# The four DeltaNet rounds of a two-layer trunk, laid out anew between the weight units

## The chip, the core and the metric

One core of one Trainium2 chip runs the whole kernel. The time is device microseconds of one execution; the median of three runs before is 2995.3 us (2992.6 to 3002.73). Engines: TensorE (PE), VectorE (DVE), ScalarE (ACT), GpSimd (POOL), and SP, which asks for the weights.

## The reference

A decoder trunk of two layers over 256 tokens and 2048 features, float32. Layer 0 mixes with mLSTM and retention, layer 1 with a gated DeltaNet; each layer ends with a SwiGLU, and each product with weights is a (256 x 2048 or wider) by (weights) matmul. The change lies in layer 1's mixer. Cut to what matters:

```python
proj = h @ w_in                                   # q, k, v (8192 columns), z, gates
qkv = silu(causal_depthwise_conv(qkv, conv_w))    # width 4
q, k = l2norm(q) * GD ** -0.5, l2norm(k)          # 16 heads of 128; v has 32
decay = exp(where(causal, g_cum[:, None] - g_cum[None, :], -inf))
a = where(strict, (k_beta @ k.T) * decay, 0)
u, w = triangular_solve(a, [v * beta, k_beta * exp(g_cum)])
attn = where(causal, (q @ k.T) * decay, 0)
# state from chunk to chunk: v_new = u - w s; out = q_g s + attn v_new
o = head_rmsnorm(out) * norm_w * silu(z);  return o @ w_out
```

## The kernel before

**Weights.** All weight products are made of 928 units. A unit is 256 rows x 512 columns of a weight matrix. SP loads it into one of four buffers `wraw`; ScalarE rounds it into `whi` (L948), VectorE takes the rest into `wlo` (L1372), and TensorE makes 12 matmuls of 512 columns: eight with `whi` (L536, L537), four with `wlo` (L542). ScalarE and VectorE may be three units ahead of TensorE at most. Eight units make a block of 512 output columns in layer 1's input projection; it has 24 blocks, 192 units, of which 16 blocks give k, q and v and 8 give z.

**Rounds.** The DeltaNet part is done for 8 value heads at a time, in four rounds, between the units of this projection. Round r begins at unit `ROUND_AT[r]` and has slots s = 0, 1, 2, ...: the function `gdn(r, s)` of each engine holds what the slot does. TensorE runs slot s right after unit `ROUND_AT[r] + s`. ScalarE and VectorE run it after their part of the unit two later (`AHEAD = 2`). So the order of work on every engine is written out by hand, and a slot that waits on another engine holds back the units behind it.

**What a round does, in slots of before.** 0 to 4: k's columns are turned (`conv_transposes`, L589), tapped (L1169) and convolved (`conv`, L1719, twelve VectorE operations), decays are summed (L749), exponentiated (L1186) and turned (L756, L1190); k is turned back (`token_major`, L742), its squares summed (L1180), k k^T formed (L763) and masked (L1729). 5, 6: the triangular systems A (`system`, L1736). 7, 12, 17: the convolutions of q and both halves of v. 8 to 19: the inversion of the 32 x 32 diagonal blocks (`leaf`, L1754 and L1757, 31 steps of two small VectorE operations, each step behind the one before; start L1743, end L1761, L1764). 9, 11, 14: q k^T, its mask, and its product into `ET` (L1809). 22 to 27: two levels of block inversion (`level_q`, `level_t`, `level_tt`, all through `per_head`, L769; copies L1204; subtractions L1769). 28 to 36: values, state and outputs, squares of the output (L1290), its norm (L1863). Both PSUM tensors `aux[0]` and `aux[1]` are shared by all of this; the four other banks hold the weight products. GpSimd makes the level masks (`level_part`, L490), zeroes T and TT, copies the leaves into T (L504), and stores each round's output to HBM; ScalarE loads it back in the last round. z blocks follow: `z_out` applies SiLU, `gate(n)` on VectorE multiplies it with the round's output.

## Time and profile before

| | |
|---|---|
| median of three runs | 2995.3 us |
| profiled execution | 2994.38 us, span 2992.6 us |
| TensorE / VectorE / ScalarE / GpSimd busy | 96% / 53% / 46% / 4% |
| chain that ended last | TensorE 84%, VectorE 9%, ScalarE 4% |
| mean granted TensorE clock | 0.981 of full speed |

Read it so: busy time is the union of an engine's instructions; a TensorE matmul's end is modelled, so its row says 0.39 us while the next starts 0.23 later. The granted clock is a share of 2.4 GHz. Idle time of an engine other than TensorE costs nothing by itself here.

### The profile page before, as it was taken

What the parts mean: (1) busy time and instruction counts of PE and PEld (TensorE: products, weight loads), DVE (VectorE), ACT (ScalarE), POOL (GpSimd) and SP (SyncE); (2) the same over time, 40 slices, a digit from 0 to 9 for tenths busy, and PEclk for the clock granted to TensorE, in tenths of its full rate; (3) what the DMA queues carried; (4) which work ended last, traced back from release to release, by engine and by line L of the source; (5) the groups of instructions that cost most, each with busy time, mean ns of one, the idle gap of its engine ahead of it and who ended that gap; (6) DMA issues with size and microseconds to landing.
All of it is one profiled execution on the core that took longest, in us unless ns stands there. A gap on an engine that the chain in (4) does not pass through costs nothing.

```text
span 2992.6 us, 37024 instructions
## 1 busy us (share of the span) xinstructions
PE 2860.9 (96%) x13396; PEld 2369.6 (79%) x13396; DVE 1586.1 (53%) x1934; ACT 1378.9 (46%) x1874; POOL 118.3 (4%) x75
## 2 busy tenths in 40 slices
PE   8999989999999999998989898899999999999998
PEld 6788768888888788876868787787888888887886
DVE  4544555544544454467484847655545544544444
ACT  5444445444444344464555637454445444443433
POOL 0000000000000000020120111000000000000000
PEclk9999989999999999999999999999999999999999
DMA  7464546666666566544434434454566666665654
GB/s 237 144 192 145 156 142 188 190 189 189 188 191 182 176 189 189 172 141 120 120 113 127 114 109 130 150 167 153 185 185 195 189 190 189 189 189 176 191 191 145
DMA packets 261265, 502.74 MB, mean 168 GB/s; under 512 B 20112, under 2 KB 20368, under 8 KB 260624
## 3 DMA queue, kind: packets, MB, share of 16 engines
q1 hardware_dynamic: 259504, 494.73, 55.0%
q0 software_dynamic: 816, 3.15, 0.3%
q10 hardware_dynamic: 816, 3.15, 0.3%
q8 instruction: 80, 1.31, 0.2%
q14 instruction: 49, 0.40, 0.0%
HBM read 495.72 MB, written 5.24 MB: 167 GB/s over the span
## 4 chain that ended last, share of the span: by engine, by line
PE 84%; DVE 9%; ACT 4%; issue 2%; DVEq 2%; DMA 0%; ACTq 0%; SPq 0%
PE acc L536 25%; PE acc L542 25%; PE acc L537 25%; PE aux L769 4%; DVE wlo L1372 2%; PE aux L589 2%; DVE arena L1757 1%; DVE arena L1754 1%; DVE const L1719 1%; DVE arena L1719 1%; ACT whi L948 1%; DVEq L1756 1%; DVEq L1723 0%; ACT arena L1290 0%; ACT aux L1180 0%
## 5 line engine op out<-in xcount | busy, mean ns | idle before, releaser
L1372 DVE TENSOR_TENSOR wlo<-wraw,whi 128x1024 fp32r<-128x1024 f32 x928 | 1151.7, 1246 | 1151.3 <-ACT whi L948 1143.6
L948 ACT ACTIVATE whi<-wraw 128x1024 fp32r<-128x1024 f32 x928 | 975.1, 1061 | 1102.4 <-PE acc L542 1048.4
L536 PE MATMUL acc<-whi,hT_hi 128*128 128x512 f32 x2624 | 1047.3, 399 | 7.5 <-ACT whi L948 7.1
L537 PE MATMUL acc<-whi,hT_lo 128*128 128x512 f32 x2624 | 1029.7, 392 | 0.0
L542 PE MATMUL acc<-wlo,hT_hi 128*128 128x512 f32 x2624 | 710.6, 393 | 42.7 <-DVE wlo L1372 42.7
L542 PEld LDWEIGHTS acc<-wlo,hT_hi 128*128 128x128 f32 x2624 | 492.9, 189 | 157.5 <-DVE wlo L1372 55.4
L536 PEld LDWEIGHTS acc<-whi,hT_hi 128*128 128x128 f32 x2624 | 497.7, 190 | 110.6 <-issue 8.8
L537 PEld LDWEIGHTS acc<-whi,hT_lo 128*128 128x128 f32 x2624 | 497.6, 190 | 102.7 <-issue 1.9
L536 PE MATMUL acc<-whi,arena 128*128 128x512 f32 x1088 | 431.1, 396 | 13.8 <-ACT whi L948 5.3
L537 PE MATMUL acc<-whi,arena 128*128 128x512 f32 x1088 | 428.9, 394 | 0.0
L542 PE MATMUL acc<-wlo,arena 128*128 128x512 f32 x1088 | 295.2, 393 | 0.0
L536 PEld LDWEIGHTS acc<-whi,arena 128*128 128x128 f32 x1088 | 206.6, 190 | 59.3 <-issue 5.5
L537 PEld LDWEIGHTS acc<-whi,arena 128*128 128x128 f32 x1088 | 206.8, 190 | 45.4
L542 PEld LDWEIGHTS acc<-wlo,arena 128*128 128x128 f32 x1088 | 205.8, 189 | 45.3
L769 PEld LDWEIGHTS aux<-arena,arena 128*128 128x128 f32 x960 | 114.0, 193 | 5.3 <-issue 2.6
L769 PE MATMUL aux<-arena,arena 128*128 128x128 f32 x960 | 114.6, 276 | 1.1 <-ACT arena L1255 1.1
L478 POOL COPY x<-xs 128x1024 f32 x16 | 19.2, 1198 | 2257.2 <-DVE xs L1410 2257.2
L964 ACT ACTIVATE arena<-acc,rstd 128x512 f32<-128x512 f32 x120 | 75.5, 684 | 15.6 <-PE acc L542 11.4
L589 PE MATMUL aux<-const,arena 128*128 128x128 f32 x240 | 32.4, 284 | 16.8 <-DVE arena L1524 9.8
L490 POOL TENSOR_TENSOR arena<-arena,const 128x1024 f32<-128x1024 f32 x16 | 41.8, 2635 | 137.0 <-DVE arena L1736 136.1
L589 PEld LDWEIGHTS aux<-const,arena 128*128 128x128 f32 x240 | 28.7, 146 | 21.9 <-DVE arena L1524 10.3
L1754 DVE TENSOR_TENSOR arena<-arena,arena 128x126 f32<-128x126 f32 (+22 forms) x124 | 39.7, 320 | 7.2 <-issue 0.4
(231 smaller groups left out, 1190.6 us busy)
## 6 DMA issues: line engine op xcount, KB each, us to landing
wraw<-in_l_w_in SPq DMA_DIRECT2D x304, 512.0 KB, 3.8
wraw<-in_l_w_gate SPq DMA_DIRECT2D x176, 512.0 KB, 3.7
wraw<-in_l_w_up SPq DMA_DIRECT2D x176, 512.0 KB, 3.7
wraw<-in_l_w_down SPq DMA_DIRECT2D x176, 512.0 KB, 4.4
wraw<-in_l_w_out SPq DMA_DIRECT2D x96, 512.0 KB, 4.6
o_rounds<-arena POOLq DMA_DIRECT2D x3, 1024.0 KB, 4.9
arena<-o_rounds ACTq DMA_DIRECT2D x3, 1024.0 KB, 5.1
x<-in_x SPq DMA_DIRECT2D x4, 512.0 KB, 6.0
```

The source lines that it names most:

```text
L490: nc.gpsimd.tensor_tensor(dst[:, c], A_[:, c], mask, ALU.mult).then_inc(part_set, 1)
L536: nc.tensor.matmul(pair[m], hi[:, k, tok], wh, start=first, stop=False)
L537: nc.tensor.matmul(pair[m], lo[:, k, tok], wh, start=False, stop=False)
L542: mm = nc.tensor.matmul(pair[m], hi[:, k, m * P:(m + 1) * P], wl, start=False, stop=k_last)
L589: mm = nc.tensor.transpose(dst[:, t * SEQ + m * P:t * SEQ + (m + 1) * P], src(m, t), ident)
L769: mm = nc.tensor.matmul(to[:, head(h)], left(h), right(h), start=True, stop=True)
L948: nc.scalar.activation(whi[:, s, :], wraw[:, s, :], ACT.Copy).then_inc(hi_done, 1)
L964: a = nc.scalar.activation(dst(m), acc[parity][:, m, :], func, scale=rstd[:, m:m + 1])
L1372: V.tensor_tensor(wlo[:, s, :], wraw[:, s, :], whi[:, s, :].bitcast(F32), ALU.subtract).then_inc(lo_done, 1)
L1719: a = V.scalar_tensor_tensor(dst[:, t, lag:], src[:, t * SEQ:(t + 1) * SEQ - lag], conv_w[:, w, CW - 1 - lag:CW - lag], dst[:, t, lag:], o ...
L1754: V.tensor_tensor(p, lead[:, j, j + 1:].unsqueeze(2).to_broadcast([P, rows, cols]), leaf_t[:, j:j + 1, 0:cols].to_broadcast([P, rows, cols ...
L1756: dve.drain()
```

## The change

Rounds begin at units 20, 57, 94 and 131 and have up to 43 slots, so a round's last slots lie over the first ones of the next. The order of the projected blocks, and of the convolutions, becomes k, first half of v, q, second half of v. In the first half of a round only k and the first half of v are convolved; the leaf inversion takes slots 10 to 20 with three steps each and nothing beside them. The convolution of q moves to slot 21, that of the second half of v to 27, q k^T and its mask to 25, the product into ET to 26. The level products now all use `aux[1]`, one a slot, each behind the subtraction of the one before; `aux[0]` is used for q and v beside them. GpSimd makes its second level mask after it has copied the leaves. The mask of k k^T moves from slot 4 to 6, A from 5 and 6 to 7 and 8. Values, state and output follow at 32 to 36, squares at 38, the root at 40, the norm at 41. The outputs of rounds 0 and 1 are loaded back to other addresses, at slots 9 and 27 of the last round, the transposed outputs of the rounds lie in another order, and the output projection takes rows of its weights in the order of `OUT1_W`. z blocks 1 and 3 are read at other units (147, 165 for 150, 163), and the first four gates follow `Z_GATED`. The core of the diff:

```diff
 Z_BLOCK = 16
+Z_GATED = [146, 149, 164, 167, 173, 181, 189]
 
 GDN_GATE_STEPS = ["raw", "exp", "log1p", "sums", "sums_exp", "neg"]
 GATE_AT = {s: i + 1 for i, s in enumerate(GDN_GATE_STEPS)}
 
 
-ROUND_AT = [23, 59, 95, 131]
-ROUND_SLOTS = 40
-
-K, Q, V0, V1 = range(4)
+ROUND_AT = [20, 57, 94, 131]
...
-TOK_AT = counts(K, Q, V0, V1)
+TOK_AT = counts(K, V0, Q, V1)
 GRAM_AT = counts("kk", "kq")
 ROOT_AT = counts("k", "q")
 LEAF_AT = counts("T", "TT")
 PART_AT = counts((32, 0), (32, 1), (64, 0), (64, 1))
-LEVEL_PSUM = counts("q32_0", "q32_1", "T32_0", "TT32_0", "T32_1", "TT32_1", "q64_0", "q64_1", "TT64_0", "TT64_1")
+LEVEL_PSUM = counts("q32_0", "q32_1", "TT32_0", "T32_0", "TT32_1", "T32_1", "q64_0", "TT64_0", "q64_1", "TT64_1")
 LEVEL_COPY = counts("q32_0", "q32_1", "q64_0", "q64_1")
-LEVEL_SUB = counts("T32_0", "TT32_0", "T32_1", "TT32_1", "TT64_0", "TT64_1")
+LEVEL_SUB = counts("TT32_0", "T32_0", "TT32_1", "T32_1", "TT64_0", "TT64_1")
 END_PSUM = counts("vn0", "s", "o0", "ks", "qs", "vn1", "o1")
...
-        o_z = [at(0, [P, M, HV * GD]), at(8 * KB, [P, M, HV * GD]), at(40 * KB, [P, M, HV * GD]), o_r]
+        o_z = [qkv[:, :, 0:HV * GD], qkv[:, :, HV * GD:], at(40 * KB, [P, M, HV * GD]), o_r]
         o_dram = nc.dram_tensor("o_rounds", (SEQ, VH * GD), F32, kind="Internal").ap()
 
         O_ORDER = [0, 2, 1, 3]
+        O_AT = [3, 1, 2, 0]
+        OUT1_W = [HV * r + t for r in O_ORDER for t in range(HV)]
+        OUT1_O = [HV * O_AT[r] + t for r in O_ORDER for t in range(HV)]
         oT_hi = at(0, [P, 2 * KT, SEQ], F32R)
...
-                pool.wait_ge(diag_set, r + 1)
-                pool.drain()
-                level_part(1, B64)
                 pool.wait_ge(leaf_set, LEAF_AT(r, "T"))
                 for b in range(4):
                     pool.drain()
                     a = nc.gpsimd.tensor_copy(T[quarter(b), :, :, quarter(b)].rearrange("p c h j -> p (c h) j"), leaf_T[quarter(b), :, :])
                 a.then_inc(t_in, 1)
+                pool.wait_ge(diag_set, r + 1)
                 pool.drain()
+                level_part(1, B64)
...
                     if r:
-                        pe.wait_ge(end_act, END_ACT(r - 1, "vn1"))
+                        pe.wait_ge(end_dve, END_DVE(r - 1, "o1"))
                     else:
                         pe.wait_ge(gate_step, GATE_AT["sums_exp"])
+                    decays(0, aux[1])
+                    if r:
+                        pe.wait_ge(end_act, END_ACT(r - 1, "vn1"))
                     conv_transposes(K, aux[0])
-                    if r:
-                        pe.wait_ge(end_dve, END_DVE(r - 1, "o1"))
-                    decays(0, aux[1])
-                if s == 1:
+                if s == 2:
                     pe.wait_ge(d_exp, D_AT(r, 0))
                     decays(1, aux[1])
-                if s == 2:
+                if s == 4:
                     pe.wait_ge(d_exp, D_AT(r, 1))
                     decays_turned(0, aux[1])
-                if s == 3:
                     pe.wait_ge(conv_sum, TOK_AT(r, K))
                     token_major(K, aux[0])
+                if s == 5:
                     pe.wait_ge(et_copy, D_AT(r, 0))
                     products(4, aux[1])
-                if s == 4:
+                if s == 7:
                     pe.wait_ge(gram_mask, GRAM_AT(r, "kk"))
                     decays_turned(1, aux[1])
-                if s == 5:
-                    pe.wait_ge(et_copy, D_AT(r, 1))
-                    conv_transposes(Q, aux[1])
-                if s == 9:
                     pe.wait_ge(tok_copy, TOK_AT(r, K))
-                    token_major(Q, aux[0])
-                    pe.wait_ge(conv_sum, TOK_AT(r, Q))
-                    products(0, aux[1])
-                if s == 10:
-                    pe.wait_ge(tok_copy, TOK_AT(r, Q))
                     conv_transposes(V0, aux[0])
                 if s == 13:
-                    pe.wait_ge(gram_mask, GRAM_AT(r, "kq"))
-                    conv_transposes(V1, aux[1])
-                if s == 15:
                     pe.wait_ge(conv_sum, TOK_AT(r, V0))
                     token_major(V0, aux[0])
-                if s == 21:
+                if s == 15:
                     pe.wait_ge(tok_copy, TOK_AT(r, V0))
-                    token_major(V1, aux[0])
-                if s == 22:
-                    pe.wait_ge(conv_sum, TOK_AT(r, V1))
+                    conv_transposes(Q, aux[0])
+                if s == 23:
+                    pe.wait_ge(et_copy, D_AT(r, 1))
                     pe.wait_ge(part_set, PART_AT(r, (32, 0)))
                     pe.wait_ge(tt_in, r + 1)
                     level_q(B32, 0, aux[1])
-                if s == 23:
-                    pe.wait_ge(tok_copy, TOK_AT(r, V1))
+                if s == 24:
                     pe.wait_ge(part_set, PART_AT(r, (32, 1)))
-                    level_q(B32, 1, aux[0])
-                if s == 24:
+                    pe.wait_ge(lev_copy, LEVEL_COPY(r, "q32_0"))
+                    level_q(B32, 1, aux[1])
+                    pe.wait_ge(conv_sum, TOK_AT(r, Q))
+                    token_major(Q, aux[0])
+                if s == 25:
                     pe.wait_ge(t_in, r + 1)
-                    pe.wait_ge(lev_copy, LEVEL_COPY(r, "q32_0"))
+                    pe.wait_ge(lev_copy, LEVEL_COPY(r, "q32_1"))
+                    level_tt(0, aux[1])
+                    pe.wait_ge(tok_copy, TOK_AT(r, Q))
+                    products(0, aux[0])
+                if s == 26:
+                    pe.wait_ge(lev_sub, LEVEL_SUB(r, "TT32_0"))
                     level_t(0, aux[1])
-                    pe.wait_ge(lev_copy, LEVEL_COPY(r, "q32_1"))
-                    level_tt(0, aux[0])
-                if s == 25:
+                    pe.wait_ge(gram_mask, GRAM_AT(r, "kq"))
+                    conv_transposes(V1, aux[0])
+                if s == 27:
                     pe.wait_ge(lev_sub, LEVEL_SUB(r, "T32_0"))
+                    level_tt(1, aux[1])
+                if s == 28:
+                    pe.wait_ge(lev_sub, LEVEL_SUB(r, "TT32_1"))
                     level_t(1, aux[1])
-                    pe.wait_ge(lev_sub, LEVEL_SUB(r, "TT32_0"))
-                    level_tt(1, aux[0])
-                if s == 26:
+                if s == 29:
                     pe.wait_ge(part_set, PART_AT(r, (64, 0)))
                     pe.wait_ge(lev_sub, LEVEL_SUB(r, "T32_1"))
                     level_q(B64, 0, aux[1])
-                    pe.wait_ge(part_set, PART_AT(r, (64, 1)))
-                    pe.wait_ge(lev_sub, LEVEL_SUB(r, "TT32_1"))
-                    level_q(B64, 1, aux[0])
-                if s == 27:
+                if s == 30:
                     pe.wait_ge(lev_copy, LEVEL_COPY(r, "q64_0"))
                     level_tt(0, aux[1])
...
                     a.then_inc(diag_set, 1)
-                if s == 8:
-                    silu(Q)
-                if s == 9:
-                    act.wait_ge(tok_tr, TOK_AT(r, Q))
-                    squares(Q, 24)
-                    nc.scalar.activation(small(2, 32, 8), small(2, 24, 8), ACT.Sqrt, bias=epsc[:, 1:2], scale=float(GD)).then_inc(root_set, 1)
-                if s == 10:
-                    tap(V0, aux[0])
-                if s == 14:
+                    if r == ROUNDS - 1:
+                        act.wait_ge(conv_tr, TOK_AT(r, V0))
+                        load_o(0)
+                if s == 11:
                     silu(V0)
-                    if r == ROUNDS - 1:
-                        act.wait_ge(conv_tr, TOK_AT(r, V1))
-                        act.wait_ge(o_stored, 16 * r)
-                        load_o(0)
-                        load_o(1)
+                if s == 13:
+                    value_rows(V0)
                 if s == 15:
-                    value_rows(V0)
-                    tap(V1, aux[1])
-                if s == 20:
-                    silu(V1)
+                    tap(Q)
+                if s == 21:
                     act.wait_ge(leaf_set, LEAF_AT(r, "TT"))
                     act.wait_ge(tt_zero, r + 1)
                     for b in range(4):
                         a = nc.scalar.activation(TT[quarter(b), :, :, quarter(b)].rearrange("p c h j -> p (c h) j"),
                                                  leaf_TT[quarter(b), :, :], ACT.Copy)
                     a.then_inc(tt_in, 1)
-                if s == 21:
-                    value_rows(V1)
-                if s == 22:
+                if s == 23:
                     act.wait_ge(t_in, r + 1)
                     level_copy("q32_0", 0, aux[1])
-                if s == 23:
-                    level_copy("q32_1", 1, aux[0])
-                if s == 25 and r == ROUNDS - 1:
+                    silu(Q)
+                if s == 24:
+                    level_copy("q32_1", 1, aux[1])
+                    act.wait_ge(tok_tr, TOK_AT(r, Q))
+                    squares(Q, 24)
+                    nc.scalar.activation(small(2, 32, 8), small(2, 24, 8), ACT.Sqrt, bias=epsc[:, 1:2], scale=float(GD)).then_inc(root_set, 1)
+                if s == 26:
+                    tap(V1)
+                if s == 27 and r == ROUNDS - 1:
+                    load_o(1)
                     load_o(2)
-                if s == 26:
+                if s == 29:
                     level_copy("q64_0", 0, aux[1])
-                    level_copy("q64_1", 1, aux[0])
-                if s == 28:
+                    silu(V1)
+                if s == 30:
+                    act.wait_ge(et_set, r + 1)
+                    value_rows(V1)
+                if s == 31:
...
                     qkv_out(b - 1)
-                if j == 3 and b > Z_BLOCK and b != Z_BLOCK + 2:
+                if j == (5 if b == Z_BLOCK + 4 else 3) and b > Z_BLOCK:
                     z_out(b - Z_BLOCK - 1)
-                if j == 6 and b == Z_BLOCK + 2:
-                    z_out(1)
                 rounds(gdn, w - AHEAD)
                 if w - AHEAD in O_SLOTS:
...
                     dve.drain()
+                if s == 7:
                     system(0)
-                if s == 6:
+                if s == 8:
                     system(1)
-                if s == 7:
-                    conv(Q, aux[1])
-                if s == 8:
+                if s == 9:
+                    conv(V0)
+                if s == 10:
                     leaf_start()
-                    leaf(0, 2)
-                if s == 9:
-                    leaf(2, 5)
-                if s == 10:
-                    leaf(5, 8)
-                if s == 11:
-                    masked("kq", 1, kqm)
-                    leaf(8, 10)
-                if s == 12:
-                    conv(V0, aux[0])
-                if s == 13:
-                    leaf(10, 14)
-                if s == 14:
+                if 10 <= s <= 20:
+                    leaf(max(0, 3 * (s - 10) - 1), 3 * (s - 10) + 2 if s < 20 else LEAF - 1)
+                if s == 20:
...
+                if s == 21:
+                    conv(Q)
+                if s == 25:
+                    dve.wait_ge(lev_psum, LEVEL_PSUM(r, "TT32_0"))
+                    level_sub(TT, 0, aux[1], 32, 1)
+                    masked("kq", aux[0], 1, kqm)
+                if s == 26:
+                    dve.wait_ge(lev_psum, LEVEL_PSUM(r, "T32_0"))
+                    level_sub(T, 0, aux[1], 32, 0)
+                    dve.wait_ge(gram_mask, GRAM_AT(r, "kq"))
                     for c in range(M):
                         dve.wait_ge(et_copy, D_AT(r, c))
                         e = ET[:, c].rearrange("p (k e) n -> p k e n", e=2)
                         a = V.tensor_tensor(e, e, kqm[:, c].unsqueeze(2).to_broadcast([P, HQ, 2, P]), ALU.mult)
                     a.then_inc(et_set, 1)
-                if s == 15:
-                    leaf(14, 18)
-                if s == 16:
-                    leaf(18, 23)
-                if s == 17:
-                    conv(V1, aux[1])
-                if s == 18:
-                    leaf(23, 27)
-                if s == 19:
-                    leaf(27, 31)
-                    leaf_end()
-                if s == 24:
-                    dve.wait_ge(lev_psum, LEVEL_PSUM(r, "TT32_0"))
-                    level_sub(T, 0, aux[1], 32, 0)
-                    level_sub(TT, 0, aux[0], 32, 1)
-                if s == 25:
+                if s == 27:
                     dve.wait_ge(lev_psum, LEVEL_PSUM(r, "TT32_1"))
+                    level_sub(TT, 1, aux[1], 32, 1)
+                    conv(V1)
+                if s == 28:
+                    dve.wait_ge(lev_psum, LEVEL_PSUM(r, "T32_1"))
                     level_sub(T, 1, aux[1], 32, 0)
-                    level_sub(TT, 1, aux[0], 32, 1)
-                if s == 27:
+                if s == 30:
                     dve.wait_ge(lev_psum, LEVEL_PSUM(r, "TT64_0"))
                     level_sub(TT, 0, aux[1], 64, 1)
+                if s == 32:
                     dve.wait_ge(lev_psum, LEVEL_PSUM(r, "TT64_1"))
-                    level_sub(TT, 1, aux[0], 64, 1)
-                if s == 29:
+                    level_sub(TT, 1, aux[1], 64, 1)
+                if s == 33:
                     dve.wait_ge(end_psum, END_PSUM(r, "o0"))
...
                     next(gates, None)
-                if j == 5 and b > Z_BLOCK + 2:
-                    gate(b - Z_BLOCK - 1)
-                if b == Z_BLOCK + 2 and j == 5:
-                    gate(0)
-                if b == Z_BLOCK + 3 and j == 0:
-                    gate(1)
+                if w in Z_GATED:
+                    gate(Z_GATED.index(w))
                 rounds(gdn, w - AHEAD)
                 if w - AHEAD in O_SLOTS:
```

On ScalarE the same slots follow (cut above): `exps` at 0 and 2, `silu(K)` at 3, `turned(0)` and the squares of k at 4, its root at 5, `tap(V0)` at 7, `diag` at 9, `silu(V0)` at 11, `tap(Q)` at 15, the copies into TT at 21, `silu(Q)` at 23, q's squares and root at 24, `tap(V1)` at 26, `silu(V1)` at 29.

## Rows read from the trace of the kernel before

**Rows 1.** The page: busy us, share of the span, instructions.
```profile
PE 2860.9 (96%) x13396; PEld 2369.6 (79%) x13396; DVE 1586.1 (53%) x1934; ACT 1378.9 (46%) x1874; POOL 118.3 (4%) x75
```

**Rows 2.** Windows: three rounds, last round, part of a second half, a low-clock stretch.
```profile
core 0: us, PE busy (x) PEld busy (x) DVE busy (x) ACT busy (x) POOL busy (x), PEclk, DMA share, GB/s
1297.60:1802.50 504.90, 457.97 (x2474) 384.57 (x2474) 318.29 (x585) 275.37 (x545) 73.17 (x41) 0.97 0.39 115
1802.50:1975.50 173.00, 154.71 (x825) 129.37 (x824) 111.75 (x202) 93.92 (x184) 20.14 (x12) 0.95 0.44 134
1570.00:1634.00 64.00, 64.00 (x414) 57.71 (x414) 24.99 (x31) 30.17 (x70) 6.63 (x3) 1.00 0.37 108
1534.90:1538.30 3.40, 2.89 (x9) 2.40 (x10) 2.73 (x10) 1.36 (x2) 0.00 (x0) 0.50 0.51 148
```

**Rows 3.** Waits of TensorE in the rounds: us in total, times, longest us.
```profile
PE acc L542 <- DVE wlo L1372: 40.4, 26, 3.1
...
PE aux L742 <- ACT arena L1175: 12.0, 4, 4.8
PE aux L756 <- DVE arena L1729: 11.7, 4, 3.0
```

**Rows 4.** Timeline of TensorE: start us, us, engine, line, operation, tiles, count, [idle before].
```profile
1482.49 1.07 PE L742 MATMUL aux<-const,arena 128*128 128x128 f32 x8
1483.39 1.97 PE L763 MATMUL aux<-arena 128*128 128x128 f32 x16
1485.12 0.47 PE L536 MATMUL acc<-whi,hT_hi 128*128 128x512 f32 x1
...
1535.41 2.08 PE L542 MATMUL acc<-wlo,hT_hi 128*128 128x512 f32 x4 [3.02 <-DVE wlo L1372]
...
1541.40 0.39 PE L536 MATMUL acc<-whi,hT_hi 128*128 128x512 f32 x1
...
1544.12 0.39 PE L536 MATMUL acc<-whi,hT_hi 128*128 128x512 f32 x1
...
1642.75 1.88 PE L749 MATMUL aux<-arena,const 128*128 128x512 f32 x4
```

**Rows 5.** Groups of ScalarE in the second round, 1466.1 to 1634.7 us.
```profile
L1290 ACT ACTIVATE arena<-arena 128x128 f32<-128x128 f32 x16 | 4.7, 296 | 3.0 <-DVE arena L1846 2.9
L1180 ACT ACTIVATE aux<-aux 128x128 f32<-128x128 f32 x16 | 4.2, 262 | 0.8 <-PE aux L742 0.7
...
L1220 ACT ACT_TABLE_LOAD x1 | 1.3, 1283 | 0.0
```

**Rows 6.** Groups of VectorE in the second round, 1466.1 to 1634.7 us.
```profile
L1372 DVE TENSOR_TENSOR wlo<-wraw,whi 128x1024 fp32r<-128x1024 f32 x37 | 46.4, 1254 | 44.0 <-ACT whi L948 42.8
L1757 DVE TENSOR_TENSOR arena<-arena,arena 128x126 f32<-128x126 f32 (+22 forms) x31 | 10.1, 325 | 2.3
L1754 DVE TENSOR_TENSOR arena<-arena,arena 128x126 f32<-128x126 f32 (+22 forms) x31 | 10.0, 321 | 1.7
L1719 DVE SCALAR_TENSOR_TENSOR arena<-aux,arena,arena 128x255 f32<-128x255 f32 (+2 forms) x24 | 9.9, 475 | 0.3
...
L1736 DVE SCALAR_TENSOR_TENSOR arena<-arena,gate_t,arena 128x128 f32<-128x128 f32 x16 | 4.4, 348 | 0.3 <-issue 0.3
...
L1743 DVE STREAM_TRANSPOSE arena<-arena 128x1024 f32<-128x1024 f32 x1 | 2.0, 2006 | 0.0
...
L1761 DVE STREAM_TRANSPOSE arena<-arena 128x512 f32<-128x512 f32 x1 | 1.1, 1150 | 0.1
```

**Rows 7.** Timelines of GpSimd and VectorE where the leaf inversion starts.
```profile
1512.57 4.72 POOL L490 TENSOR_TENSOR arena<-arena,const 128x1024 f32<-128x1024 f32 x2 [0.24 <-issue]
...
1512.69 2.29 DVE L1754 TENSOR_TENSOR arena<-arena,arena 128x31 f32<-128x31 f32 x1
1515.05 2.31 DVE L1757 TENSOR_TENSOR arena<-arena,arena 128x31 f32<-128x31 f32 x1
1517.44 0.19 DVE L1754 TENSOR_TENSOR arena<-arena,arena 128x30 f32<-128x30 f32 x1
```

More of the change, by code:

```diff
@@ L139 @@
 Z_BLOCK = 16
+Z_GATED = [146, 149, 164, 167, 173, 181, 189]
 GDN_GATE_STEPS = ["raw", "exp", "log1p", "sums", "sums_exp", "neg"]
 GATE_AT = {s: i + 1 for i, s in enumerate(GDN_GATE_STEPS)}
[L145 to L148 removed]
+ROUND_AT = [20, 57, 94, 131]
+ROUND_SLOTS = 43
+K, V0, Q, V1 = range(4)
 def counts(*steps):
@@ L398, in first_units, with phase @@
                                  col_block(w, col)[:, 2 * j:2 * j + 2, :]).then_inc(raw_in[j], 16)
-            def phase(name, n_body, lo, hi, cols):
+            def phase(name, n_body, lo, hi, cols, tiles=range(64)):
                 upb = UPB[name]
@@ L444, in _ @@
             phase("dn0", 2, 0, 2, lambda i: [(A["l0_w_down"], i * 2 * NB + b * NB) for b in range(2)])
-            l1_cols = [c for r in range(ROUNDS) for c in (2048 + 512 * r, 512 * r, 4096 + 1024 * r, 4096 + 1024 * r + NB)]
+            l1_cols = [c for r in range(ROUNDS) for c in (2048 + 512 * r, 4096 + 1024 * r, 512 * r, 4096 + 1024 * r + NB)]
             l1_cols += [8192 + NB * n for n in range(2 * ROUNDS)]
@@ L457, in _ @@
                     unit(w1, UNIT0["l1"] + b * UPB["l1"] + j, j, col)
-            phase("out1", 2, 0, 2, lambda i: [(A["l1_w_out"], i * 2 * NB + b * NB) for b in range(2)])
+            phase("out1", 2, 0, 2, lambda i: [(A["l1_w_out"], i * 2 * NB + b * NB) for b in range(2)], OUT1_W)
             phase("gu1", 2, 0, FF // NB, lambda i: [(A["l1_w_gate"], i * NB), (A["l1_w_up"], i * NB)])
@@ L543, in lo_products, with gemm_block @@
                 return mm
-            def gemm_block(name, base_u, base_b, hi, lo, slot0, parity, midway=None, fresh=False, between=None):
+            def gemm_block(name, base_u, base_b, hi, lo, slot0, parity, midway=None, fresh=False, between=None, tiles=range(64)):
                 upb = UPB[name]
@@ L554, in gemm_block @@
                     for kk in range(2):
-                        hi_products(pair, 2 * j + kk, hi, lo, slot, kk, j == 0 and kk == 0)
+                        hi_products(pair, tiles[2 * j] + kk, hi, lo, slot, kk, j == 0 and kk == 0)
                     pe.wait_ge(lo_done, base_u + (j + 1))
                     for kk in range(2):
-                        mm = lo_products(pair, 2 * j + kk, 2 * j + kk == 2 * upb - 1, hi, slot, kk)
+                        mm = lo_products(pair, tiles[2 * j] + kk, 2 * j + kk == 2 * upb - 1, hi, slot, kk)
                     mm.then_inc(unit_used, 1)
@@ L591, in transposes, with body @@
                 return mm
-            def body(name, i, n_body, hi, lo, midways, fresh=(), between=None):
+            def body(name, i, n_body, hi, lo, midways, fresh=(), between=None, tiles=range(64)):
                 for b in range(n_body):
@@ L597, in body, with residual_phase @@
                                i * (n_body // 2) + (BLOCK0[name] + b) // 2, hi, lo, b * upb, b % 2,
-                               midways[b], b in fresh, between)
+                               midways[b], b in fresh, between, tiles)
             xs_tile = lambda m, t: xs[:, m, t * P:(t + 1) * P]
             prod_tile = lambda m, t: prod[:, m, t * P:(t + 1) * P]
-            def residual_phase(name, hi, lo, transposed):
+            def residual_phase(name, hi, lo, transposed, tiles=range(64)):
                 done = 4 * (NORM_OF[name] - 1)
```

99 lines of the change are left out of this document (54 added, 45 removed).

## Prediction

> **What bounds the kernel now.** I read the page first, then the windows, then the waits, then single stretches of the timeline. TensorE is busy 96% of the span [rows 1], so no other engine's sum matters; what matters is where TensorE stands still or runs slowly. The change touches the DeltaNet rounds alone, so I cut the span there. Four rounds of 36 weight units follow each other from 1297.6 to 1975.5 us: 504.9 us for the first three and 173.0 for the last [rows 2], 677.9 in all. While they last the granted clock averages 0.97 and 0.95 [rows 2].
>
> What would these four rounds cost with no wait at the high clock? One unit of 12 matmuls starts at 1541.40 and the next at 1544.12: 2.72 us [rows 4]. Eight small transposes take 0.90 us (1482.49 to 1483.39), sixteen small records 1.73 (1483.39 to 1485.12), one decay product pair 1.7 (four records, 1.88 with the tail of the last) [rows 4]. By the code a round has 10 groups of eight, 19 of sixteen and 2 decay pairs: 9.0 + 32.9 + 3.4 = 45.3 us. So a round costs 36 x 2.72 + 45.3 = 143.2 us, four cost 572.8, and 677.9 - 572.8 = **105.1 us are lost**. That is the most that a reordering can give.
>
> Where is it lost? TensorE waits 40.4 us for the VectorE split `wlo` of a weight unit, 11.7 for the mask of k k^T, 12.0 for the SiLU before q is turned [rows 3]. That is 64.1. The low clock is most of the rest: 0.03 and 0.05 below 1 over 504.9 and 173.0 us mean about 47 us at half rate, of which half is lost, some 24 us. The clock stands at 0.50, which is 1.2 GHz, right behind waits of some 3 us, as after the one that ended at 1535.41 [rows 2, 4]. And the loss sits in one place: from 1570 to 1634 us, the second half of a round, TensorE is busy 64.00 of 64.00 us at clock 1.00 while VectorE is busy 25.0 of them [rows 2]. In the first half VectorE has 3 convolutions, the whole leaf inversion, two masks and the product on ET; in the second almost nothing.
>
> **The change part by part.** I write unit n for unit n of its round, t = 0 for a stated event. TensorE needs `wlo` of a unit 1.82 us after the unit starts (8 of its 12 matmuls come first, 8 x 0.227).
>
> *Work moved, none removed.* No matmul, activation or vector operation is added or dropped in sum. TensorE's 143.2 us a round stay, so this part is worth 0, and all that counts is which waits remain.
>
> *VectorE between slots 9 and 23.* Prices: a split 1.25 by its row, 1.13 from start to start since ends and starts overlap by 0.1; the twelve operations of a convolution 5.0 after the same overlap (12 x 0.475 = 5.7 less 11 x 0.06); eight of a system 2.1; the leaf's start 2.4 with a small copy; its end 1.9 with a second transposition that I take at 0.7 [rows 6]. A leaf step is 0.64 by the mean of 31: 10.1 + 10.0 busy and 4.0 of idle between, less the 4.2 explained below. Steps at the ends are far narrower (0.19 an operation, [rows 7]), so those in the middle must be above the mean: I take 0.75 there and 0.55 at the ends. In the changed order the mask frees TensorE in slot 7, t = 0. VectorE then does small work and split 9 until 2.1, system and split 10 until 5.4, system and split 11 until 8.6 (eight operations each, 2.1), convolution V0 and split 12 until 14.8, leaf start, two steps and split 13 until 18.9, then three steps and a split per unit: 21.9, 25.0, 28.4, 31.8, 35.2, 38.5, 41.8, 44.9, 47.8 for units 14 to 22, the leaf's end and split 23 at 51.8, convolution Q and split 24 at 58.0. TensorE would want them, each delayed by what was lost before: unit 12 loses 0.3 us, 13 loses 1.4, units 17 to 22 lose 0.2 + 0.7 + 0.6 + 0.6 + 0.4 + 0.2, unit 23 loses 1.3, slot 23 (the copies into TT, four on ScalarE behind the leaf's end) 0.5, unit 24 loses 1.2. Sum 7.4 us. VectorE is still the slower engine here (3.4 us a unit against 2.72), but by tenths at each unit, not by 3 us at a time.
>
> *The start of a round.* The tail of a round (37 to 41) now lies over slots 0 to 4 of the next, so ScalarE has there: sixteen squares (4.7 busy, some 5 with their drains), two square roots with table loads (1.28 and a short operation each), exps, taps, SiLU(K), and the eight squares of k (half of 4.2, some 2.3 with a drain) [rows 5]. Run down in order from slot 0, SiLU(K) is ready 1.5 us after TensorE asks in slot 4, and the mask 0.9 after slot 7 asks. Before, the mask alone cost 11.7 / 4 = 2.9 a round and q's SiLU 3.0 [rows 3]. Sum here 2.4. SP is moved past nothing; the weight columns are asked for in the order in which the blocks are used, with the same 512 KB each.
>
> *The level chain, slots 23 to 33.* It now alternates product and subtraction on one PSUM buffer, each product waiting for the subtraction before it, with convolution V1, both masks' rest and ET in between. Laid out by hand, unit after unit, only slot 29 waits, 0.5 us; elsewhere the subtraction (0.7) is done 0.5 us and more before it is asked for. A bound from the other side: if every one of the seven subtraction waits cost 1 us, 28 us in all.
>
> *GpSimd's second level mask.* It moves from the leaf's start to the leaf's end. From 1512.57 it runs 4.72 us, and VectorE's two operations on 31 columns inside that stretch take 2.29 and 2.31 us where those on 30 columns take 0.19 [rows 7]: 4.2 us of VectorE per round go there. The trace thus shows one engine stopping the other. The Trainium skill (SBUF - State Buffer, section "SBUF: two separate sides") says the same as a rule, that VectorE operations with two SBUF inputs and GpSimd operations hold one shared port pair for their whole length; by it the collision moves, since split 24 has two SBUF inputs as well. The sum above is without the 4.2. In its new place the mask meets split 24 or 25: between 0 and 2.4 us (one mask), I take 1.2.
>
> *The clock.* One low period of 3.4 us [rows 2] costs 1.7; before there are about 47 / 3.4 = 14 of them. Waits are now mostly under 2 us. Between 0 and 3 a round, I take 0.9 of one, 1.5 us.
>
> *Rounds 0 and 3.* Round 0 has no tail over its start: 2.4 less. In round 3 the first two gates (1.2 each) fall in VectorE's tight stretch: 2.3 more. The gates and z blocks behind slot 173 and the order in which the output projection walks its tiles cost nothing: TensorE's 0 wait there stays, and the sum over tiles has the same terms.
>
> *Sum.* A middle round loses 7.4 + 2.4 + 0.5 + 1.2 + 1.5 = 13.0. Four: 10.6 + 13.0 + 13.0 + 15.3 = 51.9. The gain is 105.1 - 51.9 = 53.2, and 2994.4 - 53.2 = **2941 us**. The profiled execution (2994.38, of which 2992.6 is the span) is 0.9 below the median of the runs, so nothing is added for that.
>
> **The rivals.**
> *Nearly all of it goes.* If the masks do not collide, the clock never falls and VectorE's real lead is larger, a round loses 7 instead of 13: 2917. For it: the second halves of before run without any wait. Against: 3.4 against 2.72 us a unit for ten units.
> *The gain is eaten by new waits in the second half.* Each wait in the level chain 1 us, plus ScalarE's squares of q, square root and level copies in front of split 27: 28 to 36 us more: 2969 to 2977. For it: these slots go from no wait to a chain. Against: ScalarE and VectorE are half idle there [rows 2].
> *Slower: the clock stays low over the leaf.* TensorE now pauses a little at each of some ten units. If the low level held through units 12 to 22, each would take twice 2.72 = 5.4 us, the waits for splits would vanish in it (5.4 is over 3.4), and the stretch would lose 11 x 2.72 = 29.9 instead of 7.4 + 1.5; a round then loses 34.0 against 26.3 before, together 136 - 105 = 31 slower: 3025. It decides from 9 of the 11 units on (13.3 us more than forecast). Against it: after the wait of 3.0 us at 1535.41 the clock is back before 1541.40, and TensorE works at full pace through two units that follow [rows 4]. The Trainium skill (TensorE: Matmul & The Clock Gate, "A second HAM failure mode") describes the mechanism: frequent short pauses between groups of matmuls let the gate swing between its levels. By this rule the change trades few long waits for the pattern that it warns of; the trace so far bears it out in no place.
> *The change doesn't do what it says.* The blocks' order is permuted in the loads, the convolutions and the taps alike, so work is not lost; I give this no share of its own.
>
> **How the numbers follow.** Forecast (2925 to 2960) 0.66, nearly all 0.12, eaten by new waits 0.14, slower 0.08. The range takes the first three and leaves out the last and the ends of the second and third: 2914 to 2974. A measurement of this kernel can tell some 0.3%, 9 us, from no change: faster 0.88, same 0.04, slower 0.08.
>
> **What would show it.** In the changed profile the four rounds should last about 625 us. Waits of TensorE for `wlo` should fall from 40.4 to about 25 to 30 and be many and short; the wait for the mask from 11.7 to under 5; the wait for q's SiLU should be gone, with one for k's in its place, under 6. The operations on 31 columns should take 0.2 us. Low clock periods should be fewer than five. Wrong would be the prediction if waits appear on the small products between units 24 and 33, if ScalarE's split becomes what TensorE waits for, or if the clock in the rounds is under 0.97.

## The result, and the profile after

The changed kernel takes 2957.99 us (2956.22 to 2961.07, four runs) beside 2994.6 for the kernel before on the same chip: a ratio of 0.9873, interval 0.9861 to 0.9886, so 1.3% faster, some 37 us. The forecast was 2941, 53 us faster, with a range from 2914 to 2974.

| | before | after |
|---|---|---|
| profiled span | 2992.6 us | 2956.9 us |
| TensorE / VectorE / ScalarE busy | 96% / 53% / 46% | 97% / 53% / 47% |
| mean granted clock | 0.981 | 0.985 |
| input projection of layer 1, first unit to the output projection's first | 830.1 us | 792.0 us |
| everything ahead of it | 1227.2 us | 1230.6 us |
| everything behind it | 935.2 us | 934.3 us |

The last three lines come from the starts of TensorE's matmuls. The part ahead has the same code in all kernels of this study and lies between 1225.3 and 1230.6 us in their profiled executions. So I compare the **projection's duration** (the layer 1 input projection with the four rounds in it), which is free of that spread; the change is worth 38.1 us there.

Windows of the kernel after (columns as in rows 2): the first three rounds, the last, part of a second half.

```profile
core 0: us, PE busy (x) PEld busy (x) DVE busy (x) ACT busy (x) POOL busy (x), PEclk, DMA share, GB/s
1292.90:1778.10 485.20, 458.79 (x2508) 384.65 (x2507) 311.89 (x588) 277.46 (x520) 70.17 (x41) 0.99 0.43 126
1778.10:1942.30 164.20, 153.30 (x840) 127.70 (x838) 110.03 (x202) 93.64 (x184) 19.86 (x12) 0.99 0.47 145
1553.60:1614.80 61.20, 60.89 (x407) 55.03 (x405) 29.83 (x42) 29.72 (x45) 5.65 (x3) 1.00 0.34 96
```

These are 148 units and 649.4 us. By the prices of the prediction they would cost 148 x 2.72 + 4 x 45.3 = 583.8 without a wait, so **65.6 us are still lost**, after 105.1 before [rows 2]. (The prediction said that the rounds should last about 625 us; that was for 144 units. Less four units of 2.72 it is 638.5.) The second half is full as it was. Waits of TensorE over the same stretch, to be read against [rows 3]:

```profile
PE acc L545 <- DVE wlo L1373: 28.9, 28, 2.5
PE aux L745 <- ACT arena L1178: 4.3, 3, 2.2
PE aux L759 <- DVE arena L1730: 1.4, 4, 0.9
PE aux L772 <- DVE arena L1770: 1.3, 4, 0.3
PE aux L772 <- ACT arena L1248: 1.0, 3, 0.3
```

The wait for splits fell from 40.4 to 28.9, the one for the mask from 11.7 to 1.4, the one for a SiLU from 12.0 to 4.3. New are two small ones, 2.3 together, at the copies into TT and at slot 29. The waits of the second round one by one, timeline of TensorE, slots 7 to 25:

```profile
1501.03 1.20 PE L545 MATMUL acc<-wlo,hT_hi 128*128 128x512 f32 x4 [0.55 <-DVE wlo L1373]
1505.86 1.19 PE L545 MATMUL acc<-wlo,hT_hi 128*128 128x512 f32 x4 [1.81 <-DVE wlo L1373]
1522.23 1.20 PE L545 MATMUL acc<-wlo,hT_hi 128*128 128x512 f32 x4 [0.42 <-DVE wlo L1373]
1525.84 1.21 PE L545 MATMUL acc<-wlo,hT_hi 128*128 128x512 f32 x4 [0.59 <-DVE wlo L1373]
1529.14 1.20 PE L545 MATMUL acc<-wlo,hT_hi 128*128 128x512 f32 x4 [0.25 <-DVE wlo L1373]
1532.31 1.20 PE L545 MATMUL acc<-wlo,hT_hi 128*128 128x512 f32 x4 [0.15 <-DVE wlo L1373]
1539.32 1.19 PE L545 MATMUL acc<-wlo,hT_hi 128*128 128x512 f32 x4 [1.03 <-DVE wlo L1373]
1540.86 2.02 PE L772 MATMUL aux<-arena,arena 128*128 128x128 f32 x16 [0.35 <-ACT arena L1248]
1547.24 1.20 PE L545 MATMUL acc<-wlo,hT_hi 128*128 128x512 f32 x4 [2.50 <-DVE wlo L1373]
```

In order: units 12 and 13, then the leaf's pace before units 18, 19, 20 and 21 (a few tenths each), unit 23, the copies into TT, and unit 24 with 2.50, the longest. These are the places of the forecast. A wait costs more than the figure in its bracket, which counts from the modelled end of the last matmul: measured from start to start these nine cost 0.8, 2.1, 0.7, 0.9, 0.6, 0.5, 1.3, 0.6 and 2.9 us.

At the leaf's start the collision of [rows 7] is gone, 0.19 and 0.21 us in place of 2.29 and 2.31 (timelines of VectorE, then GpSimd). It is back at the leaf's end: GpSimd's mask now starts at 1541.38, under the convolution of q, and three splits behind that convolution take 5.27 us where three take 3.49 without it (below).

```profile
1503.40 0.19 DVE L1755 TENSOR_TENSOR arena<-arena,arena 128x31 f32<-128x31 f32 x1
1503.67 0.21 DVE L1758 TENSOR_TENSOR arena<-arena,arena 128x31 f32<-128x31 f32 x1
...
1539.19 5.09 DVE L1720 SCALAR_TENSOR_TENSOR arena<-aux,arena,arena 128x255 f32<-128x255 f32 x12
1544.19 5.27 DVE L1373 TENSOR_TENSOR wlo<-wraw,whi 128x1024 fp32r<-128x1024 f32 x3
```

```profile
1537.58 3.63 POOL L505 COPY arena<-arena 32x512 f32<-32x512 f32 x4 [34.58 <-DVE arena L1762]
1541.38 4.73 POOL L494 TENSOR_TENSOR arena<-arena,const 128x1024 f32<-128x1024 f32 x2 [0.16 <-issue]
```

### The profile page after: what moved, and what is told of

The parts are those of the page before. It is cut to its first block, busy times and chain, and to the rows that moved or that the text cites. A ratio compares the mean times of both kernels' runs of the same rounds, so it can differ in the third digit from the quotient of the medians.

```text
span 2956.9 us, 37031 instructions
## 1 busy us (share of the span) xinstructions
PE 2854.5 (97%) x13396; PEld 2363.4 (80%) x13396; DVE 1571.3 (53%) x1934; ACT 1378.2 (47%) x1874; POOL 115.0 (4%) x75
## 4 chain that ended last, share of the span: by engine, by line
PE 84%; DVE 8%; ACT 4%; issue 1%; DVEq 1%; DMA 0%; ACTq 0%; SPq 0%
PE acc L545 26%; PE acc L539 25%; PE acc L540 25%; PE aux L772 4%; DVE wlo L1373 3%; PE aux L592 2%; DVE const L1720 1%; DVE arena L1758 1%; ACT whi L951 1%; DVE arena L1755 1%; DVE arena L1720 1%; DVEq L1724 0%; ACT arena L1293 0%; DVEq L1757 0%; ACT aux L1183 0%
## 5 line engine op out<-in xcount | busy, mean ns | idle before, releaser
L967 ACT ACTIVATE arena<-acc,rstd 128x512 f32<-128x512 f32 x120 | 75.3, 681 | 13.5 <-PE acc L545 11.4
L1207 ACT ACTIVATE arena<-aux 128x1024 f32<-128x1024 f32 x16 | 16.4, 1027 | 60.8 <-PE aux L772 60.8
```

The lines of the kernel that those rows point to most:

```text
L967: a = nc.scalar.activation(dst(m), acc[parity][:, m, :], func, scale=rstd[:, m:m + 1])
```

## The experiments

Theory: between units 12 and 24 of a round TensorE waits for the amount of work that stands in VectorE's queue, and GpSimd's masks lengthen it. Rivals: latencies and the order of semaphores set the waits, whatever VectorE has to do; or the masks' place is hidden. All runs, with the time of the kernel before measured beside each:

| run | us | before | ratio, interval | projection |
|---|---|---|---|---|
| changed kernel | 2957.99 | 2994.6 | 0.9873 (0.9861, 0.9886) | 792.0 |
| changed kernel, once more | 2955.62 | 2995.65 | 0.9861 (0.9845, 0.9876) | 791.9 |
| its second mask back at the leaf's start | 2961.79 | 2994.14 | 0.9887 (0.9871, 0.9904) | 798.0 |
| its second mask later | 2944.15 | 2994.14 | 0.9827 (0.9811, 0.9844) | 779.8 |
| the same, once more | 2945.07 | 2995.65 | 0.9827 (0.9814, 0.9841) | 780.9 |
| kernel before, mask moved | 2986.93 | 2994.14 | 0.9976 (0.9966, 0.9986) | 823.3 |
| kernel before, short convolutions | 2980.66 | 2994.14 | 0.9949 (0.9931, 0.9967) | 816.4 |
| changed kernel, short convolutions | 2941.68 | 2997.28 | 0.9815 (0.9800, 0.9830) | 777.5 |
| changed kernel, thin leaf | 2942.39 | 2997.28 | 0.9817 (0.9802, 0.9832) | 775.3 |
| mask later, q's convolution at 22 | 2948.81 | 2997.28 | 0.9845 (0.9831, 0.9858) | 785.4 |
| the same, rounds 38 apart | 2947.09 | 2997.28 | 0.9837 (0.9824, 0.9851) | 782.6 |
| mask later, rounds 38 apart, second form | 2939.73 | 2995.65 | 0.9810 (0.9797, 0.9824) | 776.4 |

**The GpSimd part of the change undone.**

```diff
                 nc.gpsimd.memset(T[:], 0.0)
+                pool.wait_ge(diag_set, r + 1)
+                pool.drain()
+                level_part(1, B64)
...
                 a.then_inc(t_in, 1)
-                pool.wait_ge(diag_set, r + 1)
                 pool.drain()
-                level_part(1, B64)
```

> The changed kernel with one part undone: GpSimd makes its second level mask at the leaf's start again, as before the change. My theory (VectorE is what TensorE waits for between units 12 and 24, and a GpSimd mask stops VectorE's operations with two SBUF inputs for its length): the first two leaf operations go from 0.2 to 2.3 us each, so unit 13 waits 4.2 us longer; the split of unit 24 goes from 3.0 us back to 1.2, so unit 24 waits 1.8 less; with one more low clock period in some rounds this is 2.4 to 4 us a round, 10 to 16 in all: 2968 to 2974 us. Rival (the masks' place is hidden by other waits): 2956 to 2960, and the split of unit 24 still takes 3.0.

Timelines of VectorE and TensorE at the leaf's start of the second round:

```profile
1499.52 2.24 DVE L1756 TENSOR_TENSOR arena<-arena,arena 128x31 f32<-128x31 f32 x1
1501.84 2.24 DVE L1759 TENSOR_TENSOR arena<-arena,arena 128x31 f32<-128x31 f32 x1
...
1506.05 2.07 PE L546 MATMUL acc<-wlo,hT_hi 128*128 128x512 f32 x4 [5.89 <-DVE wlo L1374]
```

The mechanism is as expected: 2.24 us each, the wait of unit 13 from 1.81 to 5.89, that of unit 24 from 2.9 to 1.1 from start to start. The size is not: the projection is 6.0 us longer, less than the 10 to 16 expected, and 2961.79 us lies between the ranges of the theory and of its rival. After the long wait TensorE is so late that the waits of units 17 to 22 shrink as well (3.3 to 1.7 us in that round), and the low clock now follows unit 13 in every round but no longer unit 24 in three of them. So of the whole gain of 38 us this part brings 6; the moved convolutions and masks and the even leaf bring the rest, which no run divides further.

**The second mask later still.**

```diff
                 pool.wait_ge(diag_set, r + 1)
                 pool.drain()
+                pool.wait_ge(lev_psum, LEVEL_PSUM(r, "q32_1"))
                 level_part(1, B64)
```

> The changed kernel with GpSimd's second level mask held back until the second product of the first level has been made (slot 24), where VectorE is idle much of the time. Theory of the collision: split 24 falls from 3.0 to 1.2 us, TensorE's wait at unit 24 from 2.9 to about 1.1, nothing new is waited for: 7 us less in all, 2951, and up to 6 us more where a low clock period goes too. Rival (split 24 is slow for another cause, or the collision only moves to another split that TensorE waits for): 2955 to 2960.

> The changed kernel with GpSimd's second level mask held back until slot 24, once more and beside the changed kernel itself. If the collision is worth what the last run said, it lies 0.4 to 0.5% below it (12 to 14 us); if that was the spread between executions, under 0.2%.

> The changed kernel itself, for the two comparisons of this call: 2956 to 2960 us, its input projection 792 us give or take 1.5. If it lies outside, differences between calls of some us can't be read as effects.

Timelines of GpSimd and of VectorE, second round:

```profile
1545.59 4.74 POOL L494 TENSOR_TENSOR arena<-arena,const 128x1024 f32<-128x1024 f32 x2 [7.30 <-PE aux L773]
...
1536.26 5.08 DVE L1721 SCALAR_TENSOR_TENSOR arena<-aux,arena,arena 128x255 f32<-128x255 f32 x12
1541.26 3.49 DVE L1374 TENSOR_TENSOR wlo<-wraw,whi 128x1024 fp32r<-128x1024 f32 x3
```

Three splits in 3.49 us in place of 5.27. Measured side by side this kernel takes 2945.07 and the changed one 2955.62: 10.6 us less, just short of the 12 to 14 expected. The projection is 11 to 12 us shorter. The wait of unit 24 accounts for 1.8 a round, 7 us; the other 4 are the low clock that follows that wait in rounds 0, 2 and 3 of the changed kernel (some 1.5 us each) and does not here. Low periods elsewhere come and go between the two and about cancel. The collision is shown by putting it back and by taking it away, and its price with the low clock that it brings is 11 us.

**The same part done alone, in the kernel before.** `level_part(1, B64)` is moved behind the copies into T, as in the change.

> The kernel before with only the GpSimd part of the change: its second level mask comes after the copies of the leaves into T. Theory: the leaf's first two operations fall from 2.3 to 0.2 us, 4.2 us of VectorE go per round in the stretch in which TensorE waits for VectorE, and up to 1.8 come back where the mask meets a split behind the leaf's end: 2.4 to 4.2 a round, 2978 to 2985 us. Rival (that stretch is not bound by VectorE): 2992 to 2996.

7.2 us less, just short of what was expected (2978 to 2985); two splits behind the leaf now share 6.37 us there, so part of it is handed back.

**Less VectorE work at the same places, before and after.** In both kernels:

```diff
-                    for lag in range(1, CW):
+                    for lag in range(1, 2 if b in (Q, V1) else CW):
```

> The kernel before; left out are two of the three lags of the convolution of q and of that of the second half of v, 16 VectorE operations a round, 6.7 us, so that part of the computation is missing. Both stand in the first half of a round there. Theory (VectorE bound): most of 4 x 6.7 = 27 us goes, more with low clock periods: 2960 to 2970. Rival (waits set by the order of semaphores and by ScalarE, not by the amount of VectorE work): under 8 us, over 2986.

> The changed kernel; left out are two of the three lags of the convolution of q and of that of the second half of v, so that part of the computation is missing: the same 6.7 us of VectorE a round as were left out of the kernel before. Here q's stands right behind the leaf (slot 21) and v's in slot 27. Theory: q's 3.4 us shorten the wait of unit 24 from 2.9 to at most the 1.8 of the collision with GpSimd's mask, v's 3.4 us give nothing as VectorE has room there: 4 x 1 to 2, 2950 to 2955 us. Rival (VectorE is the limit through the whole round after the change too): 20 us or more, under 2938.

Before: 13.5 us less, half of what was expected; 2980.66 us lies between the ranges of the theory and of its rival. Both short convolutions stood in the tight stretch, but the first one had been hiding something. Timelines of GpSimd and VectorE of that run:

```profile
1499.54 5.69 POOL L490 TENSOR_TENSOR arena<-arena,const 128x1024 f32<-128x1024 f32 x2 [27.94 <-DVE arena L1736]
...
1500.50 1.65 DVE L1719 SCALAR_TENSOR_TENSOR arena<-aux,arena,arena 128x255 f32<-128x255 f32 x4
1503.15 3.16 DVE L1372 TENSOR_TENSOR wlo<-wraw,whi 128x1024 fp32r<-128x1024 f32 x1 [1.01 <-ACT whi L948]
1506.23 1.99 DVE L1743 STREAM_TRANSPOSE arena<-arena 128x1024 f32<-128x1024 f32 x1
1508.15 0.84 DVE L1745 COPY arena<-const 128x512 f32<-128x512 f32 x1
```

GpSimd's **first** mask runs for 5.69 us. Under the whole convolution, which reads PSUM and one SBUF operand, it harms nobody; with the convolution cut, the split falls under it and takes 3.16 us instead of 1.23, and the copy falls under the memset that follows the mask and takes 0.84 instead of 0.42. With 1.0 of waiting for ScalarE, 3.4 of the 6.7 us a round come back.

After: 14.5 us less in the projection, far more than the 4 to 8 expected. The wait of unit 24 goes from 2.9 to 0.6, below the collision's own 1.8: the split starts 2.4 us sooner (3.4 less 1.0 of waiting for ScalarE) and is held up while TensorE still has work. The low clock behind that wait goes with it in three rounds, slot 29's 0.6 too, and low clock periods inside the rounds fall from five to one. Both convolutions were cut in one run; the places of the waits say that q's behind the leaf brings most of the gain and v's in slot 27 only the 0.6 of slot 29. The rival, 20 us or more, does not hold either.

**The leaf's pace.**

```diff
                     for j in range(first, last):
+                        if 8 <= j < 26 and j % 3 == 2:
+                            continue
```

> The changed kernel; left out are 6 of the 31 leaf steps, one of three in each of slots 11 to 16 or so, so the inversion is wrong in part: 4.4 us of VectorE a round less. Theory: in the leaf stretch TensorE waits for the pace of VectorE (3.4 us a unit against 2.72), so the waits before units 15 to 22 and most of the 1.3 before unit 23 go, 4 to 5 us a round and 14 to 20 in all: 2938 to 2944 us. Rival (these short waits are the chip's own latency between engines and stay): over 2952.

The projection is 16.7 us shorter, as expected. In the second round the waits of units 18 to 23 are gone but for 0.3 us; those of units 12, 13 and 24 and of the copies into TT stay:

```profile
1494.06 1.20 PE L545 MATMUL acc<-wlo,hT_hi 128*128 128x512 f32 x4 [0.55 <-DVE wlo L1373]
1498.90 1.20 PE L545 MATMUL acc<-wlo,hT_hi 128*128 128x512 f32 x4 [1.82 <-DVE wlo L1373]
1529.77 2.02 PE L772 MATMUL aux<-arena,arena 128*128 128x128 f32 x16 [0.34 <-ACT arena L1248]
1536.16 2.07 PE L545 MATMUL acc<-wlo,hT_hi 128*128 128x512 f32 x4 [2.51 <-DVE wlo L1373]
```

The short waits were a matter of VectorE's amount of work, not of latency.

In this kernel and in the changed kernel with short convolutions the part behind the projection lasts 940 us instead of the 934 to 936 of all others; the difference arises in the last 90 weight units, whose code is the same in both: a unit of the last product takes 2.80 us there and 2.75 elsewhere. Why is open, and it is another reason to read the projection.

**Towards a better kernel.** All three have the late mask. First q's convolution one slot later; then the rounds 38 apart as well (everything from slot 21 on one slot later, leaf steps cut over 12 slots); then q's convolution back behind the leaf, with no leaf step in its first slot and z block 0 read at unit 142 in place of 139. The lines below are the third's; of them the first kernel has only the last change, and the second has other `LEAF_CUTS` and the convolution at slot 23.

```diff
-ROUND_AT = [20, 57, 94, 131]
-ROUND_SLOTS = 43
+ROUND_AT = [20, 58, 96, 134]
+ROUND_SLOTS = 44
+LEAF_CUTS = [0, 0, 3, 6, 8, 11, 14, 16, 19, 22, 25, 28, 31]
...
-                if s == 21:
+                if s == 22:
                     conv(Q)
```

> The changed kernel with GpSimd's second level mask later (as in the experiment before) and the convolution of q one slot later, so that the split of unit 24 comes ahead of it. Theory: the wait of 1.1 us before unit 24 goes and SiLU(q), asked for only after that unit and one product group, is still in time: 4 x 1.1 less than 2944, so 2939 to 2941. Rival (the wait moves to slot 24 or to unit 25): 2943 to 2948.

> As the last one, and rounds 38 units apart (20, 58, 96, 134) with the leaf over 12 slots, and everything behind it one slot later; gates 0 to 4 and z block 1 a few units later in the last round. Theory: VectorE's work in the stretch gets one more unit of TensorE's time, 2.72 less the split of 1.13: 1.6 us a round, 6 in all: 2933 to 2936. Rival (the waits are at single places and not in the sum of the stretch, or the last round's gates collide with the z blocks): 2939 or more.

> Rounds 38 units apart with the late second level mask; the convolution of q right behind the leaf again (slot 22 there), no leaf step in the slot that starts the leaf, and z block 0 read three units later so that its SiLU is not between the square root and SiLU(k) of the last round. Theory: slot 25's wait of 2.1 a round is gone for 1.1 at the next unit, slot 4 of the last round falls from 4.6 to about 1.3, unit 13 waits about 0.8 less: the input projection with its rounds lasts about 774 us against 779.8 with the late mask alone, the whole 5 to 6 us less than that kernel in the same call. Rival (each wait that is removed comes back a unit later, as the convolution's did): within 2 us of it.

The first was a miss for the theory (2948.81 us, 2939 to 2941 expected): the 1.1 us at unit 24 went, and slot 24 waited 2.1 for SiLU(q), its rival. The second missed too (2947.09, 2933 to 2936 expected): it carried that wait along, and in its last round slot 4 waited 3.6 us for SiLU(k), ahead of which on ScalarE z block 0 had come. Timeline of TensorE, one row of each run:

```profile
1543.09 1.06 PE L746 MATMUL aux<-const,arena 128*128 128x128 f32 x8 [1.89 <-ACT arena L1179]
```

```profile
1795.73 1.94 PE L747 MATMUL aux<-const,arena 128*128 128x128 f32 x8 [3.63 <-ACT arena L1180]
```

With both mended the third is the fastest of the study: 2939.73 us, 5.3 below the late mask alone, measured beside it, and 15.9 below the changed kernel (projection 776.4, 774 expected).

## Why the forecast was right, and where it was off

**What bounds the kernel, and the ceiling.** Right in the main. The gain lies in the projection (38.1 us there), most of it out of waits for VectorE, and is far below the ceiling of 105.1. But the ceiling, and with it the 65.6, holds some 7 us that are no loss. The price of a group of small products ended where the next unit's first matmul starts, and that matmul takes 0.32 us from start to start where it takes 0.23 without a group before it (timeline of TensorE, second round, first matmuls of units 23 and 24):

```profile
1536.31 0.40 PE L539 MATMUL acc<-whi,hT_hi 128*128 128x512 f32 x1
1536.54 0.39 PE L540 MATMUL acc<-whi,hT_lo 128*128 128x512 f32 x1
...
1542.64 0.48 PE L539 MATMUL acc<-whi,hT_hi 128*128 128x512 f32 x1
1542.96 0.40 PE L540 MATMUL acc<-whi,hT_lo 128*128 128x512 f32 x1
```

Over the slots in which TensorE waits for nothing this makes some 1.8 us a round, before the change as well as after it.

**VectorE between slots 9 and 23.** Right in place, short in size: the forecast had 7.4 us for these waits and 1.2 for the collision; the second round shows 11.0 from start to start. Units 17 to 22 cost 3.3 (2.7 forecast), unit 23 1.3 (1.3), the TT copies 0.6 (0.5). Units 12 and 13 cost 2.9 in place of 1.7. Unit 24 costs 2.9 in place of 2.4, as the collision is worth 1.8 and not 1.2.

**The start of a round.** 1.3 in slot 4 (1.5 forecast) and 0.3 in slot 7 (0.9) in the second round. In the third slot 4 costs 2.4: the copies of a projected block (two on ScalarE, 1.25 us in all) come ahead of SiLU(k) in slot 3 there, and only there, which I had not seen. Unit 3 is 0.45 longer than a bare unit in every round; that is the tail of the decay products in slot 2, which the price of 1.7 holds, and no wait.

**The level chain.** Right, 0.6 in slot 29 and nothing else; its rival does not hold.

**GpSimd's mask.** The forecast said that it collides again at split 24, took 1.2 and bounded it by 2.4; measured 1.8. What was missing is what follows from it, 11 us for the whole and not 5.

**The clock.** The sum had 0.9 low periods a round and there were five of 3.4 us in four rounds, so 6 us forecast and some 8.5 spent; the sign "fewer than five" was missed by one. They fell in rounds 0, 2 and 3 behind waits of 1.8 to 2.5 us, where the prediction had seen them behind 3 us. The rival "slower, the clock stays low over the leaf" does not hold: the granted clock is 0.99 in the rounds. The rule of the Trainium skill that stood beside it (TensorE: Matmul & The Clock Gate, "A second HAM failure mode") is not borne out by this case: the leaf stretch, units 15 to 23, ran without a low period in all four rounds. The five stand behind single longer waits, of unit 13 twice and of unit 24 three times.

**Rounds 0 and 3.** Wrong for round 0. I took 2.4 off for its free start and gave it 10.6; it lost 15.5, the missing tail being outweighed by two low clock periods, 1.0 in slot 7 and 2.0 in place of 1.3 at unit 23. Round 3 lost 18.2 (15.3 forecast). Rounds 1 and 2 lost 14.5 and 17.4 (13.0 each).

**The sum.** 65.6 lost in place of 51.9. Of the missing 13.7 us some 7 are the price of the groups told above; they stand before the change too, so they were never to be won. Some 2.5 are the low clock, and 4 are left for the waits: short ones were priced at what the queue is late, while each costs a little more from start to start, and the collision was taken from the middle of its range. So the mechanism was right and several terms were too small; that the sum still came within 17 us owes nothing to errors that cancel, as nearly all have the same sign. The rest of the gap to 2941, some 3 us, is the spread of the unchanged part ahead.

## What to carry to other kernels

When one engine bounds a kernel on average and another in stretches, lay the second one's work between fixed deadlines as a running list and look at how late it is at each: that finds the places well, but add some tenths for each short wait, and look at what else shares the stretch. Read the queue of every engine at the place to which a piece is moved: GpSimd's mask was moved out of one collision into another, and 11 us more lay in holding it back some 7 us longer. Pieces that look idle may hide others, as the long convolutions hid the first mask.

## What the runs showed of the hardware that I had not expected

The collision depends on VectorE's operand sources. Beside a GpSimd multiplication of SBUF operands, a split with two SBUF inputs took 3.0 to 3.4 us in place of 1.2 and operations of 31 columns 2.2 in place of 0.2, while convolutions with one input in PSUM kept their 5.09 us for twelve. The Trainium skill (SBUF - State Buffer, section "Who interferes with whom") states this: an operation of VectorE with at most one SBUF input, outside its two-port modes, does not contend with GpSimd. The trace agrees, with these numbers. I had used the page for the place where the mask went and not for what the convolution covered where it had been. The small copy at the leaf's start has one SBUF input, and it does wait. With short convolutions in the kernel before it took 0.84 to 0.85 in all four rounds with a memset of GpSimd over its start, and 0.70 in the last round of the kernel before itself with a mask operation over its start; in each of the five it ended 0.28 us behind the end of the GpSimd operation. Everywhere else GpSimd was idle at its start or done within 0.14 us, and it took 0.37 to 0.43. So it looks held until the operation is over. That it runs in one of the two-port modes is not shown by any run.

TensorE's clock does not answer to the length of one wait alone. In the changed kernel the wait of 2.06 us before unit 24 of the first round is followed by matmuls at 0.51 of the clock (1.2 GHz), four in 2.08 us, and the longer wait of 2.50 at the same place of the second round by matmuls at full clock, four in 1.20. With the thin leaf the wait there is 2.51, and four take 2.07:

```profile
1385.17 2.08 PE L545 MATMUL acc<-wlo,hT_hi 128*128 128x512 f32 x4 [2.06 <-DVE wlo L1373]
```

```profile
1385.10:1388.50 3.40, 3.33 (x11) 2.95 (x12) 2.29 (x3) 0.00 (x0) 0.00 (x0) 0.51 0.64 181
```

What decides between the two is left open; the runs do not tell it.
